# A two-layer decoder trunk: the layout of the tokens that layer 1 compresses, and the order of keys and values

## The chip, the cores and the metric

The kernel runs on one core of a Trainium2 chip. Its metric is the device time of one execution in microseconds. One launch does the whole computation. The kernel before has a median of 1627.54 us over 3 runs (1627.14 to 1628.72).

## The reference, cut to what matters

Two layers on 512 tokens of width 1024: layer 0 has differential attention, layer 1 native sparse attention, each followed by a gated MLP with a short convolution and by a gated embedding. The change is in the "compressed" branch of layer 1. Keys kc (rotated) and values vc of 4 groups, 64 features each, are cut into 31 overlapping blocks of 32 tokens, one every 16 tokens. Each block plus a position bias goes through a small MLP:

```
n_cmp = (S - NSA_CMP_LEN) // NSA_CMP_STRIDE + 1            # 31
cidx = arange(n_cmp)[:, None] * 16 + arange(32)[None, :]

def compress(z, pos, w1, w2):
    zb = z[:, cidx] + pos[:, None, :]
    hid = gelu(einsum('bnlgd,ldf->bngf', zb, w1))          # w1: 32 x 64 x 128
    return einsum('bngf,fd->bngd', hid, w2)                # w2: 128 x 64

k_cmp = compress(kc, ck_pos, ck_w1, ck_w2)
v_cmp = compress(vc, cv_pos, cv_w1, cv_w2)
```

All is f32. The products of weights with activations are made as three products of f32 numbers split in a high part (fp32r) and a low part; the compression itself uses plain f32 matmuls, which the trace shows as two records each.

## The kernel before, in words

TensorE works through 213 weight units of 128x1024. For each, SP loads w_raw (a ring of 2), ACT copies it to w_hi (`w_high`, L360), POOL subtracts to get w_lo (`low`, L291), and TensorE uses both (rings of 4; `features`, L1173). A raw tile is loaded again once its w_lo is done; w_high of unit u waits until TensorE has done unit u - 4. Each engine has one queue in the order of the program, and the engines meet in semaphores only.

Layer 1 begins with four units "cmp", one per group. Each leaves in PSUM bank A[g] the group's 64 key features in partitions 0 to 63 and its 64 value features in partitions 64 to 127, for 512 tokens in the columns. The fifth unit, "branch", gives the gate logits in B[2]. Then:

- DVE rotates the keys of each group (`rope`, L796 to L799: multiply, stream_shuffle, multiply, add) from the bank into KR[0:64, g, :]. After group 0 it also zeroes pads (L1001, L1003).
- ACT copies the values to VR[0:64, g, :] (L613) and, one token to the left, to VR[64:128, g, :] (L614). After it has waited for kr_done it copies KR[0:64] one token to the left into KR[64:128] (L616). So partitions 64 to 127 hold the token after that of partitions 0 to 63, and one matmul of 128 rows takes two tokens of the block.
- KR and VR have a fifth group, which holds the position bias (L608), so that bias and data go through the same matmuls.
- TensorE waits for all of KR and VR, for the weights w1 and for the pads. It then makes 16 matmuls for keys and 16 for values (L1421): the moving operand is token l, l+16, l+32, ... of each of the 5 groups, 5 x 31 = 155 columns with a step of 16 elements.
- ACT applies sigmoid to the gates (L620), then, once both results are there, the bias and gelu (L625, L626). TensorE transposes the gates (L1152, gT) and goes on with the first of the four attention groups: units B[0] to B[3], and between them `compressed_kv` (L1432, L1435) and `compressed_scores` (L1461).

Of the kernel before, what the change touches and what calls it, by code (L numbers as in the profile page):

```python
# [28 lines left out]
F32 = mybir.dt.float32  # L29
# [12 lines left out]
HEAD = 64  # L42
# [48 lines left out]
class Chain:  # L91
# [10 lines left out]
    def link(self, ins):  # L102

        self.step(ins)
        self.engine.wait_ge(self.sem, self.base + self.n)
# [16 lines left out]
def trunk(nc, x_in, w_in, const_in, gain_in, conv_in, subln_in, lam_in, pos_in, pT_in, w1_in,  # L122
          cpos_in, w2_in, out):
    ctx = ExitStack()
    with ctx:
        def sb(name, shape, dt=F32, on=ctx):
            return on.enter_context(nc.sbuf_tensor(name, shape, dt))
# [8 lines left out]
        cosT = sb("cosT", [P, SEQ])  # L136
        sinT = sb("sinT", [P, SEQ])
# [29 lines left out]
        def overlay(*parts):  # L167

            with ExitStack() as on:
                return [sb(*part, on=on) for part in parts]  # L170
# [21 lines left out]
        keep1 = [("oT1_hi", [P, KT, SEQ], F32R), ("oT1_lo", [P, KT, SEQ], F32R),  # L192
                 ("kcmp", [P, GROUPS, N_PAD], F32), ("kc", [P, GROUPS, 2, N_PAD], F32R), ("Vblk", [P, GROUPS, GHEADS * HEAD], F32),
                 ("gates", [P, TT, 3 * D // HEAD], F32)]
        (oT1_hi, oT1_lo, kcmp, kc, Vblk, gates, w1k, w1v, KR, VR, hid_k, hid_v, w2, cbias, gT, ksh, kt1, kt2) = overlay(
            *keep1, ("w1k", [P, CMP_LEN // 2, CMP_HIDDEN], F32), ("w1v", [P, CMP_LEN // 2, CMP_HIDDEN], F32),

            ("KR", [P, GROUPS + 1, SEQ], F32), ("VR", [P, GROUPS + 1, SEQ], F32),
            ("hid_k", [P, GROUPS, N_PAD], F32), ("hid_v", [P, GROUPS, N_PAD], F32),
            ("w2", [P, 2, HEAD], F32), ("cbias", [P, 2], F32), ("gT", [P, SEQ], F32),  # L200
            ("ksh", [HEAD, SEQ], F32), ("kt1", [HEAD, SEQ], F32), ("kt2", [HEAD, SEQ], F32))

        (_, _, _, _, _, _, cm, Vg, vT, Kh, Kl, Q0, Q1, Q2, Q3, gp, gpT, sc, pc, pcT, oc,
         og) = overlay(
# [18 lines left out]
        A, B = [banks_a[:, n, :] for n in range(4)], [banks_b[:, n, :] for n in range(4)]  # L223
# [17 lines left out]
        S = {n: ctx.enter_context(nc.semaphore(n)) for n in names}  # L241
# [4 lines left out]

        def side(m):
            return slice(m * HEAD, (m + 1) * HEAD)

        def xT_banks(q, t):  # L250

            return ((A[0], A[1]), (A[2], A[3]), (B[0], B[1]), (B[2], B[3]))[t] if q == 0 else (B[0], B[1])
# [92 lines left out]
        def _(act):  # L345
            chain = Chain(act, S["chain_act"])
            link = chain.link

            def signal(ins, name, value):
                ins.then_inc(S[name], 1)  # L350
                act.wait_ge(S[name], value)

            def w_high(u, i=0, per=0):

                if u >= UNITS:
                    return
                if u >= RING:
                    act.wait_ge(S["units_done"], u + 1 - RING + per * i)
                act.wait_ge(S[f"w_in{u % RAW}"], 16 * (u // RAW + 1) + 16 * (per // RAW) * i)
                act.activation(w_hi[u % RING][:, :], w_raw[u % RAW][:, :], ACT.Copy).then_inc(S["w_hi_done"], 1)  # L360
# [243 lines left out]


            for dst, src in ((w1k[:, :, :], w1_in[0, :, :, :]), (w1v[:, :, :], w1_in[1, :, :, :]), (w2[:, :, :], w2_in),
                             (KR[:, GROUPS, 0:CMP_LEN], cpos_in[0, :, :]), (VR[:, GROUPS, 0:CMP_LEN], cpos_in[1, :, :])):
                act.dma_start(dst, src).then_inc(S["cmpw_in"], 16)  # L608
            gains(4, None)
            for g in range(GROUPS):  # L610
                w_high(PLAN["cmp"] + RING + g)

                act.activation(VR[0:HEAD, g, :], A[g][HEAD:P, :], ACT.Copy).then_inc(S["shifted_done"], 1)  # L613
                act.activation(VR[HEAD:P, g, 0:SEQ - 1], A[g][HEAD:P, 1:SEQ], ACT.Copy).then_inc(S["shifted_done"], 1)  # L614
                act.wait_ge(S["kr_done"], g + 1)
                act.activation(KR[HEAD:P, g, 0:SEQ - 1], KR[0:HEAD, g, 1:SEQ], ACT.Copy)\  # L616
                    .then_inc(S["shifted_done"], 1)
            w_high(PLAN["cmp"] + RING + GROUPS)
            act.wait_ge(S["units_done"], PLAN["branch"] + 1)
            signal(act.activation(gT[:, :], B[2], ACT.Sigmoid), "gsig_done", 1)  # L620
            act.wait_ge(S["hid_done"], 2)
            act.wait_ge(S["pad_ready"], 1)
            for kv, dst in enumerate((hid_k, hid_v)):

                link(act.activation(cbias[:, kv:kv + 1], A[kv][:, GROUPS * N_CMP:GROUPS * N_CMP + 1], ACT.Copy))  # L625
                signal(act.activation(dst[:, :, 0:N_CMP], A[kv][:, 0:GROUPS * N_CMP].rearrange("p (g n) -> p g n", g=GROUPS),  # L626
                                      ACT.Gelu_apprx_tanh, bias=cbias[:, kv:kv + 1]), "gelc_done", kv + 1)
            act.wait_ge(S["gatesT_done"], 1)
            link(act.activation(gates[:, :, :], A[3].rearrange("p (t n) -> p t n", t=TT)[:, :, 0:3 * D // HEAD],
                                ACT.Copy))  # L630
# [106 lines left out]
        def _(dve):  # L737
            chain = Chain(dve, S["chain_dve"])
            link = chain.link

            def signal(ins, name, value):
                ins.then_inc(S[name], 1)
                dve.wait_ge(S[name], value)
# [49 lines left out]
            def rope(bank, dst, name, value, rows=slice(0, P), tmp=None, scale=1.0):  # L793

                s_, a_, b_ = tmp
                chain.step(dve.tensor_tensor(a_, bank[rows, :], cosT[rows, :], ALU.mult))  # L796
                link(dve.stream_shuffle(s_, bank[rows, :], [(n + 16) % 32 for n in range(32)]))
                link(dve.scalar_tensor_tensor(b_, s_, scale, sinT[rows, :], ALU.mult, ALU.mult))
                signal(dve.scalar_tensor_tensor(dst, a_, scale, b_, ALU.mult, ALU.add), name, value)  # L799
# [193 lines left out]

            for g in range(GROUPS):
                dve.wait_ge(S["units_done"], PLAN["cmp"] + g + 1)
                rope(A[g], KR[0:HEAD, g, :], "kr_done", g + 1, rows=slice(0, HEAD),
                     tmp=(ksh[:, :], kt1[:, :], kt2[:, :]))
                if g == 0:
                    for pad in (hid_k[:, :, N_CMP:N_PAD], hid_v[:, :, N_CMP:N_PAD], KR[:, GROUPS, CMP_LEN:SEQ],
                                VR[:, GROUPS, CMP_LEN:SEQ]):  # L1000
                        chain.step(dve.memset(pad, 0.0))  # L1001
                    chain.wait(0)
                    signal(dve.memset(Vblk[:, :, :], 0.0), "pad_ready", 1)  # L1003
# [142 lines left out]
        def _(pe):  # L1146
# [17 lines left out]
            def features(bank, slot, rhs_hi, rhs_lo, part=None, cols=slice(0, SEQ)):  # L1164


                steps = [(k, pas) for k in range(KT) for pas in range(3)]
                if part is not None:
                    steps = steps[8 * part:8 * part + 8]
                for k, pas in steps:  # L1170
                    w = (w_hi, w_hi, w_lo)[pas][slot]
                    r = (rhs_hi, rhs_lo, rhs_hi)[pas]
                    m = pe.matmul(bank[:, cols], w[:, k * P:(k + 1) * P], r[:, k, cols], start=(k, pas) == (0, 0),  # L1173
                                  stop=(k, pas) == (KT - 1, 2))
                return m
# [18 lines left out]
            def of_tiles(U, n, tiles, banks, lhs_hi, lhs_lo, n_k):  # L1194

                for c in range(2):
                    kk = 2 * n + c - (n_k if 2 * n >= n_k else 0)
                    for t in tiles:
                        m = tokens(banks[t], (U + n) % RING, c, lhs_hi, lhs_lo, kk, t, n_k)
                return m  # L1200
# [97 lines left out]
            for t in range(TT + 1):  # L1298
                if t < TT:
                    transposes(0, t)  # L1300
                if t:
# [3 lines left out]
                    for n in range(2):  # L1305
                        m = of_tiles(PLAN["v"], n, (t - 1,), A, nT_hi, nT_lo, KT)
# [102 lines left out]
            U = PLAN["branch"]  # L1409
            weights(U + 1)  # L1410
            features(B[2], U % RING, nT_hi, nT_lo).then_inc(S["units_done"], 1)
            pe.wait_ge(S["kr_done"], GROUPS)
            pe.wait_ge(S["shifted_done"], 3 * GROUPS)
            pe.wait_ge(S["cmpw_in"], 80)
            pe.wait_ge(S["pad_ready"], 1)

            for kv, (w1, Z) in enumerate(((w1k, KR), (w1v, VR))):
                tokens_ = Z[:, :, :].rearrange("p g (n l) -> p g n l", l=CMP_STRIDE)
                for m in range(CMP_LEN // 2):
                    l = 2 * m  # L1420
                    ins = pe.matmul(A[kv][:, 0:(GROUPS + 1) * N_CMP], w1[:, m, :],  # L1421
                                    tokens_[:, :, l // CMP_STRIDE:l // CMP_STRIDE + N_CMP, l % CMP_STRIDE],
                                    start=m == 0, stop=m == CMP_LEN // 2 - 1)
                ins.then_inc(S["hid_done"], 1)
            pe.wait_ge(S["gsig_done"], 1)
            for t in range(TT):
                m = transpose(A[3][:, tok(t)], gT[:, tok(t)])
            m.then_inc(S["gatesT_done"], 1)
# [253 lines left out]
```

## Time and profile before

| | us |
|---|---|
| median of 3 runs | 1627.54 (1627.14 to 1628.72) |
| the profiled execution | 1626.89 |
| its span in the trace | 1625.1 |
| granted TensorE clock, mean | 0.969 |
| busy: PE / DVE / ACT / POOL | 1511.1 / 815.0 / 711.6 / 577.1 |
| L1421, keys: 32 records, mean 446 ns | 8.8 |
| L1421, values: 32 records, mean 440 ns | 8.6 |

PE is TensorE's matmuls, PEld its weight loads, DVE VectorE, ACT ScalarE, POOL GpSimd, SP SyncE. Times are from the start of the span. A record's duration includes a tail that overlaps the next, so what a row of matmuls takes is read from start to start. PEclk is the clock that was granted to TensorE, 1.00 for 2.4 GHz and 0.50 for 1.2 GHz.

### The profile page before, as it was taken

Reading aid. Unit: us, or ns where it says so; the run is one execution under the profiler, and the core shown is the slowest. Engines: PE = TensorE matmul, PEld = TensorE weight load, DVE = VectorE, ACT = ScalarE, POOL = GpSimd, SP = SyncE. Lnnn points to the kernel's source line nnn. Section 1 sums busy time; section 2 is a strip of 40 time slices with the busy share of each in tenths; the row PEclk is TensorE's granted clock in tenths of the full one; section 3 lists DMA queues with packets and bytes.
Section 4 is the critical chain, followed back from the end, with each engine's and each line's share of the span. In section 5 each row is a group of like instructions: output and inputs, shape, how many; then the busy total and the mean of one; then the engine's idle time right before and its main releaser. Section 6 shows DMA issues by size and latency. Waiting matters only on the chain. (4 is left out here: it accounts for less than half of the span.)

```text
span 1625.1 us, 22951 instructions
## 1 busy us (share of the span) xinstructions
PE 1511.1 (93%) x7566; PEld 1246.5 (77%) x7566; DVE 815.0 (50%) x1233; ACT 711.6 (44%) x1245; POOL 577.1 (36%) x343
## 2 busy tenths in 40 slices
PE   6898887999999999999889898989999999999988
PEld 5766655888888888778778787878788888888877
DVE  5666665365455410155556777676364554420053
ACT  5243433454444422247436364636364444432252
POOL 3524534344454444333310101010244444444332
PEclk9988987999999999999899999999999999999999
DMA  4311010132322322232410101010133223222222
GB/s 172 122 34 53 26 52 26 66 130 90 102 91 91 102 101 94 78 119 78 158 41 14 40 14 39 13 39 13 52 117 102 92 90 103 95 99 91 91 88 81
DMA packets 35336, 125.96 MB, mean 78 GB/s; under 512 B 4304, under 2 KB 5072, under 8 KB 35024
## 3 DMA queue, kind: packets, MB, share of 16 engines
q1 hardware_dynamic: 31824, 115.88, 21.0%
q10 hardware_dynamic: 3456, 9.33, 1.6%
q8 instruction: 36, 0.59, 0.1%
q14 instruction: 20, 0.16, 0.0%
HBM read 123.09 MB, written 2.10 MB: 77 GB/s over the span
## 5 line engine op out<-in xcount | busy, mean ns | idle before, releaser
L291 POOL TENSOR_TENSOR w_lo<-w_raw,w_hi 128x1024 fp32r<-128x1024 f32 x213 | 528.4, 2483 | 918.6 <-ACT w_hi L360 918.5
L1173 PE MATMUL banks_a<-nT_hi,w_hi 128*128 128x512 f32 (+1 forms) x936 | 356.5, 381 | 3.3 <-DVE nT_lo L759 3.0
L360 ACT ACTIVATE w_hi<-w_raw 128x1024 fp32r<-128x1024 f32 x213 | 225.6, 1061 | 305.6 <-PE banks_b L1182 128.1
L1173 PE MATMUL banks_a<-nT_lo,w_hi 128*128 128x512 f32 (+1 forms) x936 | 354.0, 378 | 0.0
L1173 PE MATMUL banks_a<-nT_hi,w_lo 128*128 128x512 f32 (+1 forms) x936 | 353.5, 378 | 0.0
L1173 PEld LDWEIGHTS banks_a<-nT_hi,w_hi 128*128 128x128 f32 x936 | 180.3, 193 | 35.6 <-DVE nT_lo L759 3.9
L1173 PEld LDWEIGHTS banks_a<-nT_lo,w_hi 128*128 128x128 f32 x936 | 179.8, 192 | 31.0
L1173 PEld LDWEIGHTS banks_a<-nT_hi,w_lo 128*128 128x128 f32 x936 | 179.4, 192 | 31.4
L434 ACT ACTIVATE y<-banks_a,conv 128x512 f32<-128x512 f32 x88 | 68.7, 780 | 203.9 <-PE banks_a L1173 203.4
L809 DVE SCALAR_TENSOR_TENSOR y<-banks_a,conv,y 128x511 f32<-128x511 f32 x88 | 66.0, 750 | 177.8 <-ACT y L434 177.3
L908 DVE TENSOR_REDUCE nm<-banks_b 128x2 f32<-128x256 f32 (+2 forms) x96 | 79.1, 824 | 59.5 <-PE banks_b L1332 39.4
L820 DVE TENSOR_TENSOR hT_lo<-y,hT_hi 128x512 f32 x44 | 79.8, 1815 | 43.5 <-ACT hT_hi L445 43.5
L660 ACT ACTIVATE gp<-banks_b,nm 128x128 f32<-128x128 f32 (+3 forms) x128 | 67.6, 528 | 53.2 <-DVE nm L908 48.2
L1531 PE MATMUL banks_a<-Vg,gpT 128*128 128x128 f32 x640 | 84.6, 280 | 0.0
L769 DVE COPY y<-banks_b 128x512 f32<-128x512 f32 x16 | 11.1, 691 | 135.4 <-PE banks_b L1182 135.0
L1531 PEld LDWEIGHTS banks_a<-Vg,gpT 128*128 128x128 f32 x640 | 76.5, 192 | 0.3
L811 DVE SCALAR_TENSOR_TENSOR y<-banks_a,conv,y 128x510 f32<-128x510 f32 x88 | 65.9, 748 | 12.1
L1182 PE MATMUL banks_a<-w_hi,hT_hi 128*128 128x512 f32 x176 | 69.9, 397 | 0.0
L1182 PE MATMUL banks_b<-w_hi,hT_hi 128*128 128x512 f32 x176 | 69.5, 395 | 0.0
L1182 PE MATMUL banks_b<-w_lo,hT_hi 128*128 128x512 f32 x176 | 69.5, 395 | 0.0
L1182 PE MATMUL banks_b<-w_hi,hT_lo 128*128 128x512 f32 x176 | 69.5, 395 | 0.0
L1182 PE MATMUL banks_a<-w_lo,hT_hi 128*128 128x512 f32 x176 | 69.5, 395 | 0.0
(260 smaller groups left out, 2613.3 us busy)
## 6 DMA issues: line engine op xcount, KB each, us to landing
w_raw<-in_w SPq DMA_DIRECT2D x213, 512.0 KB, 3.2
g_pre<-in_gains ACTq DMA_DIRECT2D x6, 512.0 KB, 3.7
x<-in_x SPq DMA_DIRECT2D x4, 512.0 KB, 9.5
g_post<-in_gains ACTq DMA_DIRECT2D x4, 512.0 KB, 5.1
out<-x SPq DMA_DIRECT2D x4, 512.0 KB, 2.7
pe_raw<-in_pT ACTq DMA_DIRECT2D x2, 512.0 KB, 4.4
w1k<-in_w ACTq DMA_DIRECT2D x1, 1024.0 KB, 4.9
w1v<-in_w ACTq DMA_DIRECT2D x1, 1024.0 KB, 6.8
```

The costliest lines, as they stand in the source:

```text
L291: pool.tensor_tensor(w_lo[slot][:, :], w_raw[k % RAW][:, :], w_hi[slot][:, :].bitcast(F32), ALU.subtract).then_inc(S["w_lo_done"], 1)
L360: act.activation(w_hi[u % RING][:, :], w_raw[u % RAW][:, :], ACT.Copy).then_inc(S["w_hi_done"], 1)
L434: signal(act.activation(dst, bank[:, :], ACT.Identity, bias=conv[:, bass.ds(4 * f + 3, 1)], scale=conv[:, bass.ds(4 * f + 2, 1)]), "aff_do ...
L660: signal(act.activation(gp[:, k % 2, c, 0:n], B[2 * (k % 2) + c][:, 0:n], ACT.Exp, bias=nm[:, qt, c:c + 1], accum_out=sums[:, h % 2, qt, c ...
L769: signal(dve.tensor_copy(y0[:, t, :], B[t][:, :]), "y0_done", 4 * r + t + 1)
L809: link(dve.scalar_tensor_tensor(dst[:, 1:SEQ], bank[:, 0:SEQ - 1], conv[:, bass.ds(4 * f + 1, 1)], dst[:, 1:SEQ], ALU.mult, ALU.add))
L811: last = dve.scalar_tensor_tensor(dst[:, 2:SEQ], bank[:, 0:SEQ - 2], conv[:, bass.ds(4 * f, 1)], dst[:, 2:SEQ], ALU.mult, ALU.add)
L820: signal(dve.tensor_tensor(hT_lo[:, bass.ds(j, 1), :].rearrange("p a n -> p (a n)"), y0[:, 2 + p, :], hT_hi[:, bass.ds(j, 1), :].rearrange ...
L908: signal(dve.tensor_reduce(nm[:, qt, :], banks_b[:, b:b + 2, 0:n], AX.X, ALU.max, negate=True), negmax, step + 1)
L1173: m = pe.matmul(bank[:, cols], w[:, k * P:(k + 1) * P], r[:, k, cols], start=(k, pas) == (0, 0), stop=(k, pas) == (KT - 1, 2))
L1182: m = pe.matmul(bank[:, :], a[:, kk, tok(t)], w[:, c * HALF:(c + 1) * HALF], start=(kk, pas) == (0, 0), stop=(kk, pas) == (n_k - 1, 2))
L1531: m = pe.matmul(A[c][:, tok(qt)], gpT[:, k % 2, c, kb * P:(kb + 1) * P], Vg[:, kb, HEAD * c:HEAD * c + P], start=kb == 0, stop=kb == qt)
```

## The change

KR and VR become [128, 8, 5, 32]: token 16 n + 2 j + o of group g is in partition half o, at [j, g, n]. A matmul of token pair (2 j, 2 j + 1) so reads runs of 31 adjacent elements. The halves are written straight from PSUM: ACT with two activates of 64x256 per group for the values, DVE with two subtracts of 64x256 per group for the rotated keys. The second multiply (by cos) is written back into the bank, and the shuffle works on the product with sin in SBUF. The position loads fill [128, 8, 32] each, in 128-byte pieces, padded with zeros by the host. Values are compressed ahead of keys, each with its own wait. Core of the diff:

```diff
+        def by_token(cols, odd):
+            return cols.rearrange("p (n j o) -> p o j n", j=CMP_STRIDE // 2, o=2)[:, odd, :, :]
@@ scalar
-                             (KR[:, GROUPS, 0:CMP_LEN], cpos_in[0, :, :]), (VR[:, GROUPS, 0:CMP_LEN], cpos_in[1, :, :])):
+                             (KR[:, :, GROUPS, :], cpos_in[0, :, :, :]), (VR[:, :, GROUPS, :], cpos_in[1, :, :, :])):
                 act.dma_start(dst, src).then_inc(S["cmpw_in"], 16)
...
-                act.activation(VR[0:HEAD, g, :], A[g][HEAD:P, :], ACT.Copy).then_inc(S["shifted_done"], 1)
-                act.activation(VR[HEAD:P, g, 0:SEQ - 1], A[g][HEAD:P, 1:SEQ], ACT.Copy).then_inc(S["shifted_done"], 1)
-                act.wait_ge(S["kr_done"], g + 1)
-                act.activation(KR[HEAD:P, g, 0:SEQ - 1], KR[0:HEAD, g, 1:SEQ], ACT.Copy)\
-                    .then_inc(S["shifted_done"], 1)
+                for odd in range(2):
+                    act.activation(VR[side(odd), :, g, :], by_token(A[g][HEAD:P, :], odd), ACT.Copy)\
+                        .then_inc(S["shifted_done"], 1)
...
-            act.wait_ge(S["hid_done"], 2)
             act.wait_ge(S["pad_ready"], 1)
-            for kv, dst in enumerate((hid_k, hid_v)):
+            for n, (kv, dst) in enumerate(((1, hid_v), (0, hid_k))):
+                act.wait_ge(S["hid_done"], n + 1)
@@ vector
-                rope(A[g], KR[0:HEAD, g, :], "kr_done", g + 1, rows=slice(0, HEAD),
-                     tmp=(ksh[:, :], kt1[:, :], kt2[:, :]))
+                bank = A[g][0:HEAD, :]
+                link(dve.tensor_tensor(kt1[:, :], bank, sinT[0:HEAD, :], ALU.mult))
+                chain.step(dve.tensor_tensor(bank, bank, cosT[0:HEAD, :], ALU.mult))
+                link(dve.stream_shuffle(ksh[:, :], kt1[:, :], [(n + 16) % 32 for n in range(32)]))
+                for odd in range(2):
+                    signal(dve.tensor_tensor(KR[side(odd), :, g, :], by_token(bank, odd), by_token(ksh[:, :], odd),
+                                             ALU.subtract), "kr_done", 2 * g + odd + 1)
                 if g == 0:
-                    for pad in (hid_k[:, :, N_CMP:N_PAD], hid_v[:, :, N_CMP:N_PAD], KR[:, GROUPS, CMP_LEN:SEQ],
-                                VR[:, GROUPS, CMP_LEN:SEQ]):
+                    for pad in (hid_k[:, :, N_CMP:N_PAD], hid_v[:, :, N_CMP:N_PAD]):
@@ tensor
-            pe.wait_ge(S["kr_done"], GROUPS)
-            pe.wait_ge(S["shifted_done"], 3 * GROUPS)
+            pe.wait_ge(S["shifted_done"], 2 * GROUPS)
             pe.wait_ge(S["cmpw_in"], 80)
-            pe.wait_ge(S["pad_ready"], 1)
-
-            for kv, (w1, Z) in enumerate(((w1k, KR), (w1v, VR))):
-                tokens_ = Z[:, :, :].rearrange("p g (n l) -> p g n l", l=CMP_STRIDE)
+
+            for kv, w1, Z in ((1, w1v, VR), (0, w1k, KR)):
+                pe.wait_ge(S["kr_done"], 4 if kv else 2 * GROUPS)
                 for m in range(CMP_LEN // 2):
-                    l = 2 * m
+                    at = m // (CMP_STRIDE // 2)
                     ins = pe.matmul(A[kv][:, 0:(GROUPS + 1) * N_CMP], w1[:, m, :],
-                                    tokens_[:, :, l // CMP_STRIDE:l // CMP_STRIDE + N_CMP, l % CMP_STRIDE],
+                                    Z[:, m % (CMP_STRIDE // 2), :, at:at + N_CMP],
                                     start=m == 0, stop=m == CMP_LEN // 2 - 1)
                 ins.then_inc(S["hid_done"], 1)
             pe.wait_ge(S["gsig_done"], 1)
+            pe.wait_ge(S["pad_ready"], 1)
```

## Rows read from the trace of the kernel before

**Rows 1.** The page, part 1: busy time, share, instructions, by engine

```profile
PE 1511.1 (93%) x7566; PEld 1246.5 (77%) x7566; DVE 815.0 (50%) x1233; ACT 711.6 (44%) x1245; POOL 577.1 (36%) x343
```

**Rows 2.** Waits of PE, 776 to 850: total us, times, longest

```profile
PE banks_a L1461 <- DVE kc L1070: 4.3, 1, 4.3
PE banks_a L1421 <- DVE KR L799: 4.2, 1, 4.2
```

**Rows 3.** Time line of PE: start, length, line, operation, [idle before]

```profile
794.63 0.39 PE L1173 MATMUL banks_b<-nT_hi,w_hi 128*128 128x512 f32 x1
...
799.84 0.39 PE L1173 MATMUL banks_b<-nT_hi,w_lo 128*128 128x512 f32 x1
804.40 8.75 PE L1421 MATMUL banks_a<-KR,w1k 128*128 128x155 f32 x32 [4.17 <-DVE KR L799]
812.98 8.61 PE L1421 MATMUL banks_a<-VR,w1v 128*128 128x155 f32 x32
821.40 0.62 PE L1152 MATMUL banks_a<-ident,gT 128*128 128x128 f32 x4
```

**Rows 4.** Time line of DVE in the same stretch

```profile
783.67 0.68 DVE L796 TENSOR_TENSOR kt<-banks_a,cosT 64x512 f32<-64x512 f32 x1 [5.42 <-PE banks_a L1173]
...
785.06 2.62 DVE L798 SCALAR_TENSOR_TENSOR kt<-ksh,sinT 64x512 f32<-64x512 f32 x1
...
795.31 0.69 DVE L798 SCALAR_TENSOR_TENSOR kt<-ksh,sinT 64x512 f32<-64x512 f32 x1
...
800.93 2.71 DVE L799 SCALAR_TENSOR_TENSOR KR<-kt 64x512 f32<-64x512 f32 x1
```

**Rows 5.** Time line of POOL in the same stretch

```profile
784.74 2.40 POOL L291 TENSOR_TENSOR w_lo<-w_raw,w_hi 128x1024 fp32r<-128x1024 f32 x1 [3.73 <-ACT w_hi L360]
```

**Rows 6.** Time line of ACT in the same stretch

```profile
783.60 1.06 ACT L360 ACTIVATE w_hi<-w_raw 128x1024 fp32r<-128x1024 f32 x1 [5.06 <-PE banks_a L1173]
784.68 0.60 ACT L613 ACTIVATE VR<-banks_a 64x512 f32<-64x512 f32 x1
...
803.68 0.63 ACT L616 ACTIVATE KR<-KR 64x511 f32<-64x511 f32 x1 [2.04 <-DVE KR L799]
...
806.70 0.60 ACT L620 ACTIVATE gT<-banks_b 128x512 f32<-128x512 f32 x1
```

**Rows 7.** Windows: us, busy (x) of PE, PEld, DVE, ACT, POOL, PEclk, DMA, GB/s

```profile
806.00:808.00 2.00, 2.00 (x10) 2.00 (x9) 0.00 (x0) 1.28 (x2) 1.82 (x1) 0.50 0.00 0
...
815.00:818.00 3.00, 3.00 (x13) 2.31 (x13) 0.00 (x0) 0.00 (x0) 0.00 (x0) 1.00 0.00 0
...
856.90:857.70 0.80, 0.80 (x7) 0.72 (x6) 0.71 (x6) 0.77 (x3) 0.00 (x0) 1.00 0.00 0
...
864.00:866.20 2.20, 2.20 (x21) 2.03 (x20) 0.85 (x2) 2.06 (x5) 0.00 (x0) 1.00 0.00 0
```

**Rows 8.** Time line of PE: other f32 matmuls, adjacent columns, first attention group

```profile
856.92 1.08 PE L1488 MATMUL banks_a<-Vblk,pcT 128*128 128x256 f32 x4
857.84 0.38 PE L1152 MATMUL banks_a<-ident,gp 128*128 128x128 f32 x2
...
864.22 2.00 PE L1531 MATMUL banks_a<-Vg,gpT 128*128 128x128 f32 x16
```

**Rows 9.** DMA issues: the issue on SP's queue; size and us to landing

```profile
781.18 0.33 SPq L269 DMA_DIRECT2D w_raw<-in_w  x1
...
w_raw<-in_w SPq DMA_DIRECT2D x1, 512.0 KB, 6.9
...
w_raw<-in_w SPq DMA_DIRECT2D x1, 512.0 KB, 3.3
```

**Rows 10.** DMA packets in 784 to 785 us, and in 785 to 786 us

```profile
DMA packets 462, 0.37 MB, mean 368 GB/s; under 512 B 296, under 2 KB 401, under 8 KB 454
...
DMA packets 116, 0.44 MB, mean 439 GB/s; under 512 B 9, under 2 KB 9, under 8 KB 116
```

More of the change, by code:

```diff
@@ L194, in trunk @@
                  ("gates", [P, TT, 3 * D // HEAD], F32)]
-        (oT1_hi, oT1_lo, kcmp, kc, Vblk, gates, w1k, w1v, KR, VR, hid_k, hid_v, w2, cbias, gT, ksh, kt1, kt2) = overlay(
+        (oT1_hi, oT1_lo, kcmp, kc, Vblk, gates, w1k, w1v, KR, VR, hid_k, hid_v, w2, cbias, gT, ksh, kt1) = overlay(
             *keep1, ("w1k", [P, CMP_LEN // 2, CMP_HIDDEN], F32), ("w1v", [P, CMP_LEN // 2, CMP_HIDDEN], F32),
-            ("KR", [P, GROUPS + 1, SEQ], F32), ("VR", [P, GROUPS + 1, SEQ], F32),
+            ("KR", [P, CMP_STRIDE // 2, GROUPS + 1, N_PAD], F32), ("VR", [P, CMP_STRIDE // 2, GROUPS + 1, N_PAD], F32),
             ("hid_k", [P, GROUPS, N_PAD], F32), ("hid_v", [P, GROUPS, N_PAD], F32),
             ("w2", [P, 2, HEAD], F32), ("cbias", [P, 2], F32), ("gT", [P, SEQ], F32),
-            ("ksh", [HEAD, SEQ], F32), ("kt1", [HEAD, SEQ], F32), ("kt2", [HEAD, SEQ], F32))
+            ("ksh", [HEAD, SEQ], F32), ("kt1", [HEAD, SEQ], F32))
         (_, _, _, _, _, _, cm, Vg, vT, Kh, Kl, Q0, Q1, Q2, Q3, gp, gpT, sc, pc, pcT, oc,
@@ L620, in _ @@
             signal(act.activation(gT[:, :], B[2], ACT.Sigmoid), "gsig_done", 1)
-            act.wait_ge(S["hid_done"], 2)
             act.wait_ge(S["pad_ready"], 1)
-            for kv, dst in enumerate((hid_k, hid_v)):
+            for n, (kv, dst) in enumerate(((1, hid_v), (0, hid_k))):
+                act.wait_ge(S["hid_done"], n + 1)
                 link(act.activation(cbias[:, kv:kv + 1], A[kv][:, GROUPS * N_CMP:GROUPS * N_CMP + 1], ACT.Copy))
                 signal(act.activation(dst[:, :, 0:N_CMP], A[kv][:, 0:GROUPS * N_CMP].rearrange("p (g n) -> p g n", g=GROUPS),
-                                      ACT.Gelu_apprx_tanh, bias=cbias[:, kv:kv + 1]), "gelc_done", kv + 1)
+                                      ACT.Gelu_apprx_tanh, bias=cbias[:, kv:kv + 1]), "gelc_done", n + 1)
             act.wait_ge(S["gatesT_done"], 1)
@@ L1667 @@
                         for n, order in (("ck", perm), ("cv", np.arange(HEAD)))]),
-        "cpos": np.stack([np.concatenate([pos.T, np.roll(pos, -1, axis=0).T]) for pos in
-                          (i["nsa_ck_pos"][0][:, perm], i["nsa_cv_pos"][0])]),
+        "cpos": np.stack([np.pad(pos.reshape(2, CMP_STRIDE // 2, 2, HEAD).transpose(2, 3, 1, 0)
+                                 .reshape(P, CMP_STRIDE // 2, 2), ((0, 0), (0, 0), (0, N_PAD - 2)))
+                          for pos in (i["nsa_ck_pos"][0][:, perm], i["nsa_cv_pos"][0])]),
         "w2": np.stack([i["nsa_ck_w2"][0][:, perm], i["nsa_cv_w2"][0]], 1),
```

## The prediction

> **What bounds the kernel now.** I read the page first, for which engine the time belongs to, then the waits of TensorE around the edited stage, then the time lines of the engines there, then the clock by window and the DMA issues. TensorE is busy for 1511.1 of 1625.1 us [rows 1], so the time changes only by what leaves TensorE's own line or by a gap in it. In the stretch that holds the compression of keys and values it waits twice: 4.2 us ahead of the compression matmuls (L1421), put down to DVE's KR, and 4.3 us ahead of the first compressed scores (L1461) [rows 2]. The diff touches only what feeds and makes up the first.
>
> Its time line [rows 3]: the last matmul of unit "branch" starts at 799.84 and nothing more comes until 804.40. The 64 records of L1421 (2 per f32 matmul, 16 matmuls for keys and 16 for values) then run until the gate transposes start at 821.40: 17.00 us, 0.266 us each. The new text can act on these 4.3 us of gap and on these 17.00 us.
>
> **Why the gap is there.** The last group's projection is complete when TensorE turns to banks_b at 794.63 [rows 3]. DVE then needs the four operations of the rotation, and the last of them, which takes 0.69 us undisturbed (the row at 795.31 is the like operation L798), took 2.71 us at 800.93; L798 had 2.62 us at 785.06 [rows 4]. Both read two SBUF tiles, and both ended with a w_lo of POOL (784.74 plus 2.40 us for the one at 785.06) [rows 5]. Only then can ACT copy the rotated key one token to the left, 0.63 us from 803.68 to 804.31 [rows 6]; TensorE starts 0.09 us later.
>
> **Part 1, the rotation.** Per group DVE had multiply, shuffle, multiply, add, all of 512 columns. Now it has multiply by sin, multiply by cos back into the bank, shuffle, and two subtracts of 64x256 that write the even and the odd tokens straight to their half of KR. A multiply is 0.68 us, and from a multiply's start to the start of what follows the shuffle is 1.39 us (783.67 to 785.06) [rows 4]. A half of 256 columns lies between 0.34 (half of 0.68) and 0.68 us; I take 0.45, nearer to the half, since most of such an operation's time goes by its columns. That makes 0.72 + 1.39 + 0.90 = 3.0 us, with waits. Every multiply and subtract now has one operand in PSUM, and I take 0.68 for it beside a running w_lo too; if it were held as those with two SBUF tiles are, it would be the +1.9 us of the next sentence but one. The new shuffle reads SBUF, which no row of this kernel shows beside POOL: from nothing to +1.9 us (2.62 - 0.69); I take nothing. The last group is then ready at 794.8 + 3.0 = 797.8, with one such hold at 799.7, and its KR is asked for only after the value matmuls, at about 804.6. Cost on the path: 0; the cover is the 4.6 us of the value matmuls.
>
> The Trainium skill, "SBUF — State Buffer", section "Who interferes with whom", says that a DVE instruction with two SBUF inputs contends with a GpSimd instruction that reads SBUF, and that one with at most one SBUF input outside the two-port modes does not. By that the shuffle stays undisturbed; by the other reading KR is ready at 799.7, and the sum is the same by both.
>
> **Part 2, ACT.** Per group three activates (two of values, one copy of the key) become two of 64x256. One of 512 columns is 0.60 us (784.68) [rows 6], so each is between 0.30 and, if reading every 16th column makes them dearer, 0.60; I take 0.40. ACT no longer waits for kr_done. The last pair follows w_high of the group, which needs the projection (794.8) and its raw weights. The raw weights of the second group's w_high were issued at 781.2 and landed 6.9 us later, at 788.1; a later load takes 3.3 us [rows 9]. So that w_high is at 788.1, its w_lo at 789.2 to 791.6, the raw tile after next lands at 794.9, the last w_high is at 794.9 to 796.0 (1.06 us) [rows 6], and the last VR is written at 796.8, 3.3 us ahead of 800.1. The sigmoid of the gates, complete at 807.3 now (806.70 + 0.60) [rows 6], comes 4 us earlier with its w_high, to 803.3, and is needed at 809.
>
> **Part 3, the positions.** The two cpos loads grow from 128 pieces of 128 bytes to 1024 each: 16 pieces for each of the 16 DMA engines become 128, 112 more. The present ones move in the microsecond from 784, behind the 1 MB weight tiles; in it the 16 engines handled 462 packets, of them 296 under 512 bytes: at most 16/462 = 0.035 us each. Of full-size ones they handled 116 in the next microsecond, 0.138 us each [rows 10]. At 0.035 the 112 cost 3.9 us: landing at 789, needed at 800.1. If they delay the raw weights by all of it, VR comes at 796.8 + 3.9 = 800.7, 0.6 us of gap. I take 0 to 0.6 and put 0.1. The memsets of KR and VR go, and are off the path.
>
> **Part 4, the matmuls.** The count stays at 64 records of 155 columns. What changes is the read: the old moving operand steps by 16 elements (64 bytes), the new one reads runs of 31 adjacent ones. The clock rows say what held the old ones [rows 7]: at 806 to 808 us the granted clock is 0.50, 1.2 GHz, after the gap of 4.2 us; at 815 to 818 it is 1.00, 2.4 GHz; but the 32 records of keys (804.40 to 812.98, 0.268 us each, about half of them at the lower level) and the 32 of values (812.98 to 821.40, 0.263) cost the same [rows 3]. A matmul that does not mind half the clock is held by something else, and the read is what is peculiar to it. At 1.00 the f32 matmul with adjacent columns costs: four of 256 columns from 856.92 to 857.84, 0.230 us each; sixteen of 128 columns in 2.00 us, at most 0.125 each [rows 7, 8]. By the first, 155 columns are 0.139; between the two, 0.147. I take 0.142: 64 x 0.142 = 9.1 us. Bounds: 0.125 (a record of 128 columns) gives 8.0, and 0.263, if the step was not the cause, gives 16.8.
>
> The Trainium skill, "SBUF — State Buffer", section "Door 1: The DMA port swizzle (why `[64,N]` ≈ `[32,N]`)", has 16-byte lines in SBUF: accesses that stay in a line go at full rate, each step to a new line pays. The matmul rows above agree. It speaks against the change in one place: DVE now reads ksh at 64-byte steps. No row shows such a read on DVE; if it cost twice, a group would take 3.9 us and KR would be there at 798.7, which changes nothing in the sum.
>
> **Part 5, the order.** Values first means that the 32 value records stand on VR and on kr_done at 4 (banks 0 and 1 read), both there before 800; the keys' part of DVE's work is covered by them. pad_ready is met before 792. gelc_done at 2 comes from ACT 0.8 us after the last key record, at about 810, and is asked for after the first group unit, at about 815.
>
> **The sum**, on the profiled execution (span 1625.1, time 1626.89 us, 0.65 below the median 1627.54): the first compression matmul moves from 804.40 to 800.1 + 0.1, saving 4.2; the 17.00 us become 9.1 with 0.1 for the change of kind, saving 7.8 to 7.9. Together 12.1 us. Behind it every wait is relative to TensorE (the 4.3 us at L1461 follow from the ropes of group 0, which start when TensorE ends that unit), so the saving lasts to the end. Median 1627.5 - 12.1 = **1615.4 us**; the profiled span about 1613.0.
>
> **The rivals.**
> A, forecast, 0.80: both gap and matmul rate; own range 1613.3 to 1617.5. For: the rate that ignores the clock.
> B, 0.09: the rate is not the step's doing (the five separate runs, or the form, say), and only the gap goes. Time 1627.5 - 4.2 = 1623.3. For it: no row shows a matmul with several short runs. Against: the rows of 256 and 128 columns share everything else. A part of it, 0.20 us a record, would give 1619.1.
> C, 0.07: the wait moves to L1461 and grows, since DVE's L1065 there reads two SBUF tiles and meets POOL by chance of a few tenths; one more such meeting is 1.9 us, with its lower clock after it perhaps 3: 1618.4.
> D, the slower one, 0.03: small packets cost what large ones do and stand ahead of the raw weights. 112 x 0.138 = 15.5 us; VR at 796.8 + 15.5 = 812.3, a gap of 12.2 instead of the old 4.3, then about 18 records at the lower clock (0.26 in place of 0.142: 2.1 us). Against the 12.1 saved stand 12.2 + 2.1: 1629.7. It decides from 0.12 us a packet; the rows say 0.035. The Trainium skill, "DMA: Bandwidth & Descriptors", section "Specifications", wants 512 bytes or more for full rate and has a read-modify-write below that, which is this mechanism; by [rows 10] the trace does not bear out so high a price.
> That the change doesn't do what it says, 0.01: 1627.5.
>
> **From these the numbers**: the range 1612.8 to 1620.0 holds A, C and the partial B, some 0.88 of the chance, taken a little wide on the low side for a record nearer 0.125. Faster by over 0.2% (3.3 us, about what a measurement of this kernel can tell from no change) is A, B and C: 0.95. Within 0.2% 0.03, slower 0.02.
>
> **What would show it.** Right: L1421's values start within 0.5 us of the last record of unit "branch"; the granted clock stays 1.00 from 780 to the wait at L1461; 64 records in 8.0 to 9.6 us; ACT's last VR before 800; DVE's last KR before 804; the wait at L1461 still 4 us. Wrong: a record of L1421 near 0.26 us at clock 1.00 (B); a wait of L1421 on ACT VR, or w_high waiting for w_raw around 790 to 800 (D); L1461's wait above 6 us (C).

## The result, and the profile after

The changed kernel takes 1614.77 us (median of 4 runs, 1614.45 to 1615.66) against 1627.93 us for the kernel before (4 runs): ratio 0.992, 95% interval 0.9903 to 0.9937. The forecast was 1615.4, with a range of 1612.8 to 1620.0. The profiled execution went from 1626.89 to 1614.45 us, its span from 1625.1 to 1612.6.

The time line of TensorE after, which answers to [rows 3]:

```profile
798.48 0.40 PE L1177 MATMUL banks_b<-nT_hi,w_lo 128*128 128x512 f32 x1
798.72 4.38 PE L1423 MATMUL banks_a<-VR,w1v 128*128 128x155 f32 x32
802.93 4.38 PE L1423 MATMUL banks_a<-KR,w1k 128*128 128x155 f32 x32
807.14 0.60 PE L1156 MATMUL banks_a<-ident,gT 128*128 128x128 f32 x4
```

The compression follows unit "branch" without a gap, and the 64 records take 807.14 - 798.72 = 8.42 us, 0.132 us each. The best measure of the change is the stage from the start of the last record of unit "branch" to the gate transposes: 21.56 us before (799.84 to 821.40), 8.66 after. That is 12.90 us: 4.32 of gap and 8.58 of matmuls. The spans differ by 12.5. The stage starts 1.36 us earlier than before, which is not the edit's doing: the same record of TensorE was 2.35 us earlier already long ahead of any changed instruction (699.92 against 702.27), and that lead went down to 1.36 by the stage. Behind the stage 1.8 us are given back. The wait for the first compressed scores, behind the stage, is the same 4.3 us, as the waits of PE show (776 to 840 us; total, times, longest):

```profile
PE banks_a L1464 <- DVE kc L1074: 4.3, 1, 4.3
```

The granted clock (third figure from the end) stays at 1.00 through the stage, where it was 0.50 for part of the keys before [rows 7]. It falls only after the next wait, which starts at about 825.3 us. The windows after:

```profile
800.00:804.50 4.50, 4.50 (x36) 4.50 (x35) 0.00 (x0) 3.14 (x4) 2.36 (x1) 1.00 0.23 60
804.50:809.00 4.50, 4.50 (x33) 4.24 (x32) 0.00 (x0) 1.41 (x5) 0.00 (x0) 1.00 0.18 70
...
831.50:833.00 1.50, 1.50 (x8) 1.50 (x9) 1.47 (x2) 0.00 (x0) 0.32 (x1) 0.50 0.16 27
```

ACT after, answering to [rows 6]. The second position load and the one behind it hold its queue for 5.3 us, and its first w_high of the stage starts at 784.16, though DVE had the bank at 782.31:

```profile
778.74 2.39 ACTq L611 DMA_DIRECT2D VR<-in_cpos  x1
781.18 2.88 ACTq L386 DMA_DIRECT2D g_pre<-in_gains  x1
784.16 1.06 ACT L363 ACTIVATE w_hi<-w_raw 128x1024 fp32r<-128x1024 f32 x1 [6.44 <-issue]
...
791.26 1.06 ACT L363 ACTIVATE w_hi<-w_raw 128x1024 fp32r<-128x1024 f32 x1 [3.23 <-DMA w_raw<-in_w]
...
793.58 1.06 ACT L363 ACTIVATE w_hi<-w_raw 128x1024 fp32r<-128x1024 f32 x1 [0.58 <-DMA w_raw<-in_w]
794.55 0.77 ACT L617 ACTIVATE VR<-banks_a 64x256 f32<-64x256 f32 x2
```

The last VR is there at 795.32, 3.4 us ahead of its use. DVE's last group answers to [rows 4]:

```profile
793.74 0.68 DVE L997 TENSOR_TENSOR kt<-banks_a,sinT 64x512 f32<-64x512 f32 x1
794.46 0.69 DVE L998 TENSOR_TENSOR banks_a<-banks_a,cosT 64x512 f32<-64x512 f32 x1
...
795.07 0.74 DVE L999 STREAM_SHUFFLE ksh<-kt 64x512 f32<-64x512 f32 x1
795.85 1.22 DVE L1001 TENSOR_TENSOR KR<-banks_a,ksh 64x256 f32<-64x256 f32 x2
```

It ends at 797.07. POOL's w_lo ran from 792.40 to 797.17, beside all of these operations, and none of them took longer than its like did elsewhere.

### The profile page after: what moved, and what is told of

It is laid out like the page before. It is cut to its first block and busy times, and to the rows that moved or that the text cites. A ratio compares the mean times of both kernels' runs of the same rounds, so it can differ in the third digit from the quotient of the medians.

```text
span 1612.6 us, 22950 instructions
## 1 busy us (share of the span) xinstructions
PE 1502.7 (93%) x7566; PEld 1240.5 (77%) x7566; DVE 808.7 (50%) x1235; ACT 707.4 (44%) x1241; POOL 577.9 (36%) x343
## 5 line engine op out<-in xcount | busy, mean ns | idle before, releaser
L811 DVE SCALAR_TENSOR_TENSOR y<-banks_a,conv,y 128x510 f32<-128x510 f32 x88 | 65.9, 749 | 12.1
```

The source lines that it names most:

```text
L811: last = dve.scalar_tensor_tensor(dst[:, 2:SEQ], bank[:, 0:SEQ - 2], conv[:, bass.ds(4 * f, 1)], dst[:, 2:SEQ], ALU.mult, ALU.add)
```

## The experiments

The runs of one kernel spread by up to 10 us on some of the chips, so medians near each other don't separate terms of 1 or 2 us. The stage as measured above does, and the verdicts rest on it. It is read from one profiled execution of each kernel, but it repeats: in the seven kernels that keep the adjacent layout and have no gap (changed, after_again, keys_first, dve_forms, group_order, group_swap, group_later) it is 8.66 us each time. The whole time of the profiled executions follows it: against the changed kernel they are 12.4 us longer for 12.9 of stage (before), 10.8 for 9.5 (gap_only), 5.6 for 4.4 (rate_only) and 3.6 for 3.8 (more_pieces).

| kernel | stage, us | gap, us | us a record | median, us |
|---|---|---|---|---|
| before | 21.56 | 4.3 | 0.268, 0.263 | 1627.9 |
| changed | 8.66 | 0 | 0.132 | 1614.8 |
| gap_only (step 8) | 18.14 | 0 | 0.280 | 1622.9 |
| step_4 | 17.93 | 0 | 0.276 | 1623.3 (1 run) |
| step_2 | 9.24 | 0 | 0.141 | 1613.6 (1 run) |
| rate_only | 13.02 | 2.6 | 0.187, 0.132 | 1615.3 |
| keys_first | 8.66 | 0 | 0.132 | 1615.0 |
| more_pieces | 12.41 | 2.0 | 0.188, 0.132 | 1616.9 |

Two figures in a cell are for the first and the second 32 records. The gap is from where the next record of unit "branch" would have started (its records start 0.23 us apart).

**gap_only: the gap closed, the stepped read kept**

```diff
-("KR", [P, CMP_STRIDE // 2, GROUPS + 1, N_PAD], F32), ...
+("KR", [P, CMP_STRIDE // 2 // STEP, GROUPS + 1, N_PAD, STEP], F32), ...        # STEP = 8, VR too
...
-                                    Z[:, m % (CMP_STRIDE // 2), :, at:at + N_CMP],
+                                    Z[:, m % (CMP_STRIDE // 2) // STEP, :, at:at + N_CMP, m % STEP],
```

> The changed kernel, but the 8 token pairs of a stride lie innermost, so that the compression matmuls step by 8 elements (32 bytes) and the halves are still written straight from PSUM. The gap ahead of the matmuls stays closed, the adjacent read is undone. Theory (the 64-byte step held the old matmuls, 0.263 us a record; adjacent 0.132): a 32-byte step is as bad, 64 records in 16.8 us, time 1614.8 + 8.4 = 1623.2 us. Rival (the old rate came from where the keys were written, or from the half clock): 0.132 a record, 1614.8 us. Rival (the penalty grows with the step): something between, near 0.19 a record, 1618.6. The positions now move in 1 KB pieces: ACT's first w_high of the stage should start at about 782.4 instead of 784.2, with no effect on the end.

1622.9 us (1620.3 to 1626.9, ratio to before 0.9978, interval 0.9964 to 0.9992), and 0.280 us a record (TensorE's time line):

```profile
799.11 9.12 PE L1424 MATMUL banks_a<-VR,w1v 128*128 128x155 f32 x32
808.06 9.14 PE L1424 MATMUL banks_a<-KR,w1k 128*128 128x155 f32 x32
817.02 0.62 PE L1157 MATMUL banks_a<-ident,gT 128*128 128x128 f32 x4
```

A window in the keys shows the clock at 1.00:

```profile
812.00:814.00 2.00, 2.00 (x9) 1.50 (x8) 0.00 (x0) 0.00 (x0) 0.00 (x0) 1.00 0.00 0
```

The time is what had been expected with the step as the cause (1623.2), though a record is dearer than the 0.263 that had been taken. The step is the cause of the slow record, not the writer of the data and not the clock. The positions moved in 1 KB pieces here, and ACT's first w_high started at 782.64, as expected.

**step_4 and step_2: how far apart may the elements be**

The same edit with STEP = 4 and STEP = 2.

> As gap_only, with 4 token pairs innermost: the matmuls step by 4 elements, 16 bytes. Theory of lines of 16 bytes: every element is in a new line, so as slow as 64 bytes, 0.263 us a record, time near 1623. Rival (the penalty follows the distance): nearer 0.16 to 0.2. Of DVE: its subtracts of 64x256 read with an inner step of 2 elements in runs of 4 and should fall from 0.594 us if the step of 16 elements made them dear (0.42 is the price of 256 adjacent columns), and stay if the price lies elsewhere.

> The changed kernel with 2 token pairs innermost: the matmuls step by 2 elements (8 bytes), two elements to a line of 16 bytes. Steps of 4, 8 and 16 elements gave 0.276, 0.280 and 0.263 us a record, adjacent ones 0.132. Theory of 16-byte lines (two hits on a line are enough): near 0.132 us a record, stage as in the changed kernel. Rival (any step breaks the fast read): 0.26 to 0.28. Rival (the rate goes with the bytes passed over): about 0.2.

Steps of 4 and of 2 elements, in that order:

```profile
799.98 9.02 PE L1424 MATMUL banks_a<-VR,w1v 128*128 128x155 f32 x32
808.82 9.03 PE L1424 MATMUL banks_a<-KR,w1k 128*128 128x155 f32 x32
```

```profile
797.86 4.66 PE L1424 MATMUL banks_a<-VR,w1v 128*128 128x155 f32 x32
802.35 4.66 PE L1424 MATMUL banks_a<-KR,w1k 128*128 128x155 f32 x32
```

From the first start to the second: 8.84 us with 16 bytes between elements, 4.49 with 8, against 4.21 adjacent and 8.95 with 32 bytes. The price is a threshold between 8 and 16 bytes, not a slope. The Trainium skill, "SBUF — State Buffer", section "Door 1: The DMA port swizzle (why `[64,N]` ≈ `[32,N]`)", has 16-byte lines that need at least two accesses each for full rate. These rows agree: two f32 elements in a line are nearly enough (0.141 us a record against 0.132), one is not (0.276). The same note gives 4 f32 as how far one can step for free; read as a step of 4 elements, that is not so here.

**rate_only: the layout, but keys on the old way**

```diff
+                rope(A[g], kf[:, g, :], "kr_done", g + 1, rows=slice(0, HEAD), tmp=(ksh[:, :], kt1[:, :], kt2[:, :]))
...
+                act.wait_ge(S["kr_done"], g + 1)
+                for odd in range(2):
+                    act.activation(KR[side(odd), :, g, :], by_token(kf[:, g, :], odd), ACT.Copy)\
+                        .then_inc(S["shifted_done"], 1)
...
+            pe.wait_ge(S["shifted_done"], 4 * GROUPS)
```

> The changed kernel, but keys take the old way: the four operations of the old rotation into an SBUF tile, then two copies by ACT into the halves, and TensorE waits for all of both before it starts. The layout with adjacent tokens stays. Theory (gap and rate are separate terms): the gap of 4.2 us returns, a little longer by the second copy (4.5), and with it the lower clock, at which a record of 155 columns cannot be under 0.26 us: about 18 records at 0.26 and 46 at 0.132 make 10.8 us in place of 8.4. Time 1614.8 + 4.5 + 2.4 = 1621.7. Rival (adjacent reads also make 0.132 at the lower clock, or the clock does not fall): 1619.3. Rival (the two SBUF-fed operations of DVE no longer meet POOL in this arrangement): gap under 2 us, 1616.

1615.3 us (1609.9 to 1620.1, ratio 0.9919, interval 0.9894 to 0.9945). TensorE and the last group on DVE on the time line:

```profile
802.02 6.15 PE L1423 MATMUL banks_a<-VR,w1v 128*128 128x155 f32 x32 [2.43 <-ACT KR L622]
808.01 4.38 PE L1423 MATMUL banks_a<-KR,w1k 128*128 128x155 f32 x32
...
796.31 1.40 DVE L803 SCALAR_TENSOR_TENSOR kt<-ksh,sinT 64x512 f32<-64x512 f32 x1
797.75 2.91 DVE L804 SCALAR_TENSOR_TENSOR kf<-kt 64x512 f32<-64x512 f32 x1
```

A window in the values:

```profile
804.00:805.00 1.00, 1.00 (x6) 1.00 (x6) 0.00 (x0) 0.94 (x2) 1.00 (x1) 0.50 0.00 0
```

The gap comes back, with operations on two SBUF tiles held by w_lo (1.40 and 2.91 us in place of 0.69) and ACT's copies behind them. It is 2.6 us and not the 4.5 expected, because DVE began the last group at 794.93 instead of 798.83. Of these 3.9 us the two large memsets, which are gone, are only 1.0. Another 2.3 are holds by POOL that did not happen here (0.68 us in place of 2.62 in the first group, 0.68 in place of 1.00 in the second), and 0.64 is an earlier start. The clock falls behind the gap (0.50 in the window), and the first 32 records take 5.99 us instead of 4.21. Gap and clock, 2.6 + 1.8 us, on the 8.66 of the changed kernel make up the stage of 13.02. The forecast of 1621.7 was missed, and the medians alone do not show the gap's price: 1615.3 is 0.5 us above the changed kernel, with runs from 1609.9 to 1620.1, of which the profiled one was the slowest. What shows it is the stage.

**keys_first: the order undone**

```diff
-            for kv, w1, Z in ((1, w1v, VR), (0, w1k, KR)):
-                pe.wait_ge(S["kr_done"], 4 if kv else 2 * GROUPS)
+            for kv, w1, Z in ((0, w1k, KR), (1, w1v, VR)):
+                pe.wait_ge(S["kr_done"], 2 * GROUPS)
```

> The changed kernel with keys compressed ahead of values, TensorE waiting for all of KR first. Theory (the last KR is written 1.6 us before TensorE ends unit branch, 797.1 against 798.7, so the order is worth nothing): 1614.8 us, no gap. Rival (values first hides a late KR): a gap of the size of the lateness, above 1616. The gelu of the values then comes last; it is asked for 5 us later, so it hides too.

1615.0 us, no gap, the same 8.66 us of stage. The changed kernel, run again later (after_again), gave 1614.97.

> The changed kernel itself, to stand beside the next two on one chip, since the spread between runs is larger on some chips than the terms at stake. Expected 1614.8 us.

The order of values and keys is worth nothing here.

**dve_forms: which operand makes DVE's subtract dear**

```diff
...
+                    b_ = adjacent(bank) if g in (1, 2) else by_token(bank, odd)
+                    k_ = adjacent(ksh[:, :]) if g in (0, 2) else by_token(ksh[:, :], odd)
```

> The changed kernel, whose subtracts of 64x256 took 0.594 us reading both PSUM and SBUF at a step of 16 elements, and 0.417 with a step of 2 on both. Here group 0 reads SBUF (ksh) adjacently and PSUM by 16, group 1 PSUM adjacently and SBUF by 16, group 2 both adjacently, group 3 as in the changed kernel; so keys of groups 0 to 2 are computed from the wrong columns. Theory (the SBUF read at 64 bytes costs, as it does for the matmuls and for ACT's copies from SBUF, 0.66 us against 0.38 from PSUM): 0.42, 0.59, 0.42, 0.59. Rival (the PSUM read costs): 0.59, 0.42, 0.42, 0.59. Rival (they add): 0.5, 0.5, 0.42, 0.59. The time should stay that of the changed kernel.

With `adjacent` the subtract reads 256 columns next to each other, so the keys of groups 0 to 2 come from other columns than they should; only the durations are of use. The pairs of subtracts of groups 0 to 3:

```profile
785.61 0.87 DVE L1005 TENSOR_TENSOR KR<-banks_a,ksh 64x256 f32<-64x256 f32 x2
...
789.98 1.20 DVE L1005 TENSOR_TENSOR KR<-banks_a,ksh 64x256 f32<-64x256 f32 x2
...
793.32 0.87 DVE L1005 TENSOR_TENSOR KR<-banks_a,ksh 64x256 f32<-64x256 f32 x2
...
796.83 1.22 DVE L1005 TENSOR_TENSOR KR<-banks_a,ksh 64x256 f32<-64x256 f32 x2
```

0.87, 1.20, 0.87, 1.22 us: with ksh adjacent (groups 0 and 2) a pair costs 0.87 whether PSUM is stepped or not, with ksh stepped 0.35 more. This is what had been expected if the SBUF read costs. In gap_only and step_4, where both operands have a step of 2, the subtracts are at 0.417 us too.

**more_pieces: the rival of the small pieces, by dose**

```diff
...
+                             *((spare[:, :, n, :], cpos_in[n % 2, :, :, :]) for n in range(4))):
...
+            pe.wait_ge(S["cmpw_in"], 144)
```

> The changed kernel with four more loads of 1024 pieces of 128 bytes each, into a spare tile, behind the two that it has; TensorE waits for them too. It doses the rival of the forecast in which small pieces hold up the stage. Measured so far: a load of 1024 pieces holds ACT's queue for about 2.4 us, and the pieces themselves take 0.013 us each (1220 in a microsecond on 16 engines), 0.85 us a load. Theory (the price is ACT's queue, which stands behind the issue): 4 x 2.4 = 9.6 us later w_high of the first group, 793.8 in place of 784.2; unit branch, which wants its w_lo at 793.3, then waits about 4 us, and the VR of the last group comes about 9.6 - 3.4 (its slack) = 6 us late: stage 5 to 8 us longer plus 1 to 2 of lower clock, time 1621 to 1625. Rival (only the moving of the pieces costs): 3.4 us, which the slack covers: no change, 1615. Rival (pieces as dear as large packets, 0.138 us each): 4 x 64 x 0.138 = 35 us, time near 1645.

1616.9 us (1615.8 to 1619.0). ACT's and TensorE's time lines:

```profile
781.51 7.46 ACTq L613 DMA_DIRECT2D spare<-in_cpos  x4
...
789.78 1.06 ACT L364 ACTIVATE w_hi<-w_raw 128x1024 fp32r<-128x1024 f32 x1 [11.85 <-issue]
...
800.12 0.77 ACT L619 ACTIVATE VR<-banks_a 64x256 f32<-64x256 f32 x2
800.93 6.16 PE L1425 MATMUL banks_a<-VR,w1v 128*128 128x155 f32 x32 [1.82 <-ACT VR L619]
```

The mechanism is the one named, the issues on ACT's queue. Its size was over-estimated: four loads hold the queue for 7.46 us, not 9.6, and the load behind them goes in 0.67 us instead of 2.88, so w_high is only 5.6 us late (789.78 against 784.16). The last VR is 5.6 us late (800.89 against 795.32), 3.4 of them are slack, and what is left, with the lower clock behind it (0.188 us a record), makes the stage 3.75 us longer. The time stays below the 1621 to 1625 expected. So the changed kernel is 3.4 us from a stall by its own position loads.

**group_order, group_swap, group_later: what bounds next**

In all four attention groups TensorE waits for DVE's subtracts of Q or what follows them, and the two subtracts, which read two SBUF tiles, took 5.21 us at 818.93 in the changed kernel, beside a w_lo, against 1.41 at 827.73. These three kernels move ACT's w_high, and with it POOL's w_lo. The edit of group_order:

```diff
-                w_high(u, i, per)
                 if not first:
                     for m in range(2):
                         goT_high(2 * g - 2 + m, m)
                 query_high(0)
+                w_high(u, i, per)
+                query_high(1)
                 w_high(u + 1, i, per)
-                query_high(1)
-                w_high(u + 2, i, per)
...
+                w_high(u + 2, i, per)
                 act.wait_ge(S["units_done"], PLAN["group"] + 4 * g + 4)
```

> The changed kernel, and in each attention group ACT's three first w_high are put later: behind the high parts of the first queries, behind those of the second, and behind the low parts of the keys. Purpose: w_lo of POOL then runs beside fewer DVE operations that read two SBUF tiles (2.79 us in place of 0.69 for one multiply of the rotation, 3.63 and 5.21 in place of 1.4 for the two subtracts of Q), which stand ahead of the compressed scores, where TensorE waits 4.1 to 4.3 us in each of the 4 groups. Theory: 2 to 4 us off each wait, and where it falls under about 2 us no fall of the clock: 8 to 20 us in all, 1595 to 1607. Rival (w_lo meets other DVE operations instead, later in the group): 1611 to 1618. Rival (the later w_high holds up the exponentials, ACT's busiest stretch): slower than 1616.

1607.3 us (1606.1 to 1609.8), ratio to before 0.9876 (0.9859 to 0.9893), just above the 1595 to 1607 expected. group_swap is group_order with a swap on DVE (`goT_low` behind the subtracts of Q):

> group_order, with one swap on DVE: in groups 1 to 3 the two subtracts of Q go ahead of the two low parts of the attention output, which read PSUM and so do not mind POOL. In group_order the first w_lo of a group (896.81) still held the second subtract of Q (3.64 us for the two in place of 1.4). Theory: the wait ahead of the compressed scores falls from 2.0 to under 1 us in groups 1 to 3 and there may be no lower clock behind it: 3 to 8 us less than group_order (1607.3), so 1600 to 1604. Rival (the output's low parts are then late for the transposes that need their bank): 1607 or more.

1600.6 us (1596.2 to 1605.3), ratio 0.9837 (0.982 to 0.9854). group_later has no swap and spreads the w_high further:

> As group_order, but the first w_high of a group comes behind the high parts of the second queries, the second behind the low parts of the keys, and the third and fourth among the exponentials (behind the second and the fourth pair). The subtracts of Q then meet no w_lo either. Theory (ACT has room in the loop of exponentials): as group_swap, 1600 to 1604. Rival (ACT is the engine that TensorE waits for there, 8.0 us of waits on gpT in the changed kernel, so each microsecond put there is paid, 2 x 1.06 in 4 groups): 1607 to 1612.

1604.0 us (1603.4 to 1605.6), ratio 0.9864 (0.9847 to 0.9881). The waits of PE from 776 to 1140 us, in the changed kernel, in group_swap and in group_later:

```profile
PE banks_a L1464 <- DVE Q L1069: 12.3, 3, 4.1
PE banks_a L1156 <- ACT gpT L670: 8.0, 8, 1.8
PE banks_a L1156 <- issue: 5.8, 16, 0.8
PE banks_a L1464 <- DVE kc L1074: 4.3, 1, 4.3
```

```profile
PE banks_a L1156 <- DVE pc L1096: 8.4, 4, 2.1
PE banks_a L1156 <- issue: 4.9, 15, 0.8
...
PE banks_a L1156 <- ACT gpT L670: 3.5, 5, 2.1
PE banks_a L1156 <- ACT vT L704: 2.0, 3, 0.9
PE banks_a L1464 <- DVE Q L1066: 1.3, 3, 0.5
PE banks_a L1464 <- DVE kc L1074: 0.7, 1, 0.7
```

```profile
PE banks_a L1155 <- issue: 10.2, 16, 1.5
PE banks_a L1155 <- DVE pc L1095: 8.4, 4, 2.1
...
PE banks_a L1463 <- DVE kc L1073: 0.2, 1, 0.2
```

The 16.6 us of waits ahead of the compressed scores fall to 2.0 in group_swap, and 8.4 us come back one step later, ahead of the transposes of pc, which wait for DVE's pc. The waits for gpT fall too, from 8.0 to 3.5. All waits of the stretch together, without one of 4.2 us on xn that lies ahead of the edit, go from 30.4 to 20.8 us: 9.6, against 9.1 between the two profiled spans (1612.6 and 1603.5). The medians differ by more, 14.4 us (1614.97 for the changed kernel run beside it): the profiled run of group_swap was the slowest of its five. The other four had a mean granted clock of 0.975 to 0.978, this one 0.973 and the changed kernel 0.971, so part of the rest goes with the clock; how much was not taken apart. In group_later the waits put down to issue are 10.2 us instead of the 4.9 of group_swap. Of the two, group_swap has the lower median, but their intervals overlap a little.

## Why the prediction was right

**The total.** The stage saved 12.90 us where 12.1 had been forecast, 0.7 of the difference in the matmuls. Behind it 0.9 us went back up to the first product with Vg (below), for which the forecast had nothing. That the total came within 0.6 us is in part luck: these two nearly cancel, and the drift ahead of the stage, 1.4 us, is larger than the whole error.

**The gap (Part 1 and 2, forecast 4.2 us; measured 4.32).** That it would close, and by which operations, held. Less the 1.36 us by which TensorE is early, the forecast times are 796.4 for KR's last part and 795.4 for the last VR; measured are 797.07 and 795.32. But the account of why the gap was there leaves out what made it. The last group's operations, with their one hold, took 4.8 us. From the projection at 794.63 they would have ended at about 799.5 and the copy at about 800.1, when TensorE was just done with unit "branch". DVE was late before it began that group, as rows of the kernel before show:

```profile
788.59 0.46 DVE L1001 MEMSET KR<- 128x480 f32 x1
789.09 0.46 DVE L1001 MEMSET VR<- 128x480 f32 x1
...
796.03 2.77 DVE L799 SCALAR_TENSOR_TENSOR KR<-kt 64x512 f32<-64x512 f32 x1
798.83 0.68 DVE L796 TENSOR_TENSOR kt<-banks_a,cosT 64x512 f32<-64x512 f32 x1
```

It starts the last group at 798.83, 4.2 us after the projection. In the groups ahead w_lo had held it up by 1.9, 0.3 and 2.1 us. The two memsets shown had cost 1.0 more, so they were not off the path, as Part 3 has it. In the changed kernel none of this is left, and DVE begins its last group at 793.74. A sign named for rival D, w_high waiting for w_raw, appeared as well (3.23 and 0.58 us in ACT's rows above) without D: in gap_only, where the positions move in 1 KB pieces, ACT waits 2.38 and 2.09 us for w_raw in the same stage. It did not tell the two apart.

Two prices inside were off and both were covered. DVE's half was taken at 0.45 us and costs 0.59, since reading ksh at a step of 64 bytes costs 0.18 us a half (dve_forms). The shuffle from SBUF and the multiplies from PSUM were taken as undisturbed beside POOL, and are. What the forecast left out is the issue of the position loads: ACT's queue stands 2.39 us at one of them and 2.88 at the load behind, for which nothing had been put; ACT's idle time hid it.

**The small packets (Part 3, forecast 0.1 us; measured 0).** In the microsecond from 785 the 16 engines handled 1220 packets, 0.013 us each, against the bound of 0.035 that had been read from [rows 10]:

```profile
DMA packets 1220, 0.25 MB, mean 248 GB/s; under 512 B 1199, under 2 KB 1199, under 8 KB 1219
```

Rival D named ACT's w_high as what would be late, but by the wrong way and at the wrong price. With four more loads it is late, by the queue of ACT and not by the moving.

**The matmuls (Part 4, forecast 9.1 us; measured 8.42).** The argument from the clock, that a record which costs the same at 1.2 and at 2.4 GHz is held by its read, was confirmed by gap_only and step_4: stepped, 0.276 to 0.280 us at 2.4 GHz; adjacent, 0.132. The term was mis-sized by 0.7 us. The row of 128 columns was divided with the tail of its last record in it (2.00 us for 16), which made its 0.125 an upper end and not the lower bound that it was also used as. In the changed kernel such a row can be read from start to start:

```profile
862.09 2.00 PE L1534 MATMUL banks_a<-Vg,gpT 128*128 128x128 f32 x16
863.93 0.82 PE L1156 MATMUL banks_a<-ident,gp 128*128 128x128 f32 x6
```

That is 1.84 us for 16, 0.115 each. The row of 256 columns alone, 0.230 / 256 x 155 = 0.139, is nearer and would have given 8.9 us. Why 64 records in a row take 0.5 us less still was not followed up.

**The two terms are not independent.** Old, 21.56 us; the gap alone gives 3.42 of it (gap_only, whose step is 8 instead of 16), the rate alone 8.54 (rate_only), both 12.90, 0.94 more than their sum. Step 8's dearer records account for 0.91 of that (its 64 take 17.91 us, those of before 17.00). That the rest is next to nothing is chance: rate_only's 8.54 holds 1.7 us of the gap (2.6 left of 4.3) and lacks the 1.8 us that the lower clock cost its first 32 records, and these cancel. That clock cost was seen only for adjacent records; the stepped ones cost 0.268 us with half of them at the lower level and 0.263 at the upper [rows 3, 7].

**The order (Part 5, forecast 0; measured 0)**, by keys_first. **Rival B** (the rate is not the step's doing) fell with gap_only. **Rival C** did not happen: the wait at L1464 is 4.3 us as before, and its DVE operations are held as before (5.21 us for two). The lower clock behind it lasted longer, to about 838 us, and the first product with Vg starts 42.3 us after the gate transposes instead of 41.4, so 0.9 us went back there.

## What to carry to other kernels

When a matmul costs the same at both clock levels, look at how its moving operand is laid out. Here f32 elements 16 bytes or more apart cost twice (0.263 to 0.280 us a record against 0.132), and elements 8 bytes apart 0.141. Writing the layout straight from PSUM also removes a dependent copy, and beside POOL's w_lo DVE's operations with one operand in PSUM kept their 0.68 us, where those with two in SBUF took up to 2.91. Look also at when an engine began the work that is waited for, and not only at how long that work took. Count the DMAs of many small pieces by what they hold on the issuing engine's queue, and see where the next wait has the same cause: here DVE's subtracts met POOL in four more places, and moving them apart was worth another 14 us in the medians, some 9 between profiled runs.

## What the runs showed of the hardware that had not been expected

A step of 16 elements costs on reads from SBUF on three engines, and on no read from PSUM that was tried. ACT, 256 columns: 0.38 us from PSUM (VR, L617), 0.66 from SBUF (KR<-kf in rate_only), about as much as the 0.63 of 511 adjacent columns from SBUF [rows 6]. With a step of 2 in gap_only the PSUM read takes the same 0.38. DVE, 256 columns: 0.42 with only PSUM stepped, 0.60 with ksh stepped. A matmul of 155 columns: 0.132 adjacent, 0.263 stepped. The row of ACT in rate_only (durations min/median/max):

```profile
L622 ACT ACTIVATE KR<-kf x8: 626/658/672, 786.5 to 801.3; 64x256 f32<-64x256 f32 x8
```

A step of 8 elements (0.280 us a record) and of 4 (0.276) were dearer than the old one of 16 (0.263). That was not followed up.

A DMA of 1024 pieces of 128 bytes held ACT's queue for 2.4 us in the changed kernel (0.47 when the same bytes went in 1 KB pieces), though by 0.013 us a piece they took under 1 us to move. It was the second such load; the first, just ahead of it, held the queue for 0.70, and the load behind both, which has no small pieces, for 2.88. Why the time falls on the later ones is open.
